# Gates and branches multiplied by token, two slots a pair of 512 columns, merged branches turned for the output projection

## The reference, cut to what matters

```python
for layer in range(2):
    h = rms_norm_2(x, norm1_g[layer])
    y_sb    = stick-breaking attention of h @ w_l[...]      # 256 wide
    y_rwkv  = rwkv7 time mix of h @ w_l[...]                # 256 wide
    y_moba  = moba attention of h @ w_l[...]                # 256 wide
    y_hgrn  = hgrn2 mixer of h @ w_l[...]                   # 256 wide
    merged = None
    for n, y_n in enumerate((y_sb, y_rwkv, y_moba, y_hgrn)):
        gate = sigmoid(h @ w_l[:, GATE_OFF + n * 1024 : GATE_OFF + (n + 1) * 1024])
        term = gate * (y_n @ w_branch[layer, n])            # (256, 256) @ (256, 1024)
        merged = term if merged is None else merged + term
    x = x + merged @ w_out[layer]                           # (256, 1024) @ (1024, 1024)
    h2 = rms_norm_2(x, norm2_g[layer])
    x = x + (silu(h2 @ w_ffn_gate) * (h2 @ w_ffn_up)) @ w_ffn_down
```

## Time and profile before

| | |
|---|---|
| median of three runs | 1333.72 us (1331.26 to 1333.73) |
| the profiled execution | 1330.48 us, of it the span 1328.7 us |
| PE busy | 1282.2 us (97%), 10548 matmuls |
| PEld busy | 1160.2 us (87%) |
| DVE busy | 837.4 us (63%) |
| ACT busy | 692.6 us (52%) |
| POOL busy | 118.6 us (9%) |
| DMA | 222.93 MB, 168 GB/s on average |
| mean granted clock of PE | 0.992 of full speed |

### The profile page before, as it was taken

How to read it: one execution, slowest core, us unless ns; L and a number is a source line. 1 busy time by engine, 2 the same in 40 slices (tenths; PEclk the granted TensorE clock), 3 DMA queues, 4 the chain that set the end, 5 groups by cost and what they waited for, 6 DMA issues and landing times.

```text
span 1328.7 us, 24883 instructions
## 1 busy us (share of the span) xinstructions
PE 1282.2 (97%) x10548; PEld 1160.2 (87%) x10548; DVE 837.4 (63%) x1257; ACT 692.6 (52%) x894; POOL 118.6 (9%) x77
## 2 busy tenths in 40 slices
PE   5999999999999999999999999999999999999997
PEld 4998898889999999989888888999999889888886
DVE  3567756886656977656655544556878756755533
ACT  2455536765766566244544434766567335544432
POOL 0000000000001330232000000000430130100000
PEclk9999999999999999999999999999999999999999
DMA  9766745724434433124555554434443114555552
GB/s 387 261 255 258 288 181 177 257 85 159 157 128 159 159 128 127 66 96 159 189 178 176 186 190 158 150 136 142 150 154 127 65 67 160 206 176 178 185 167 86
DMA packets 35102, 222.93 MB, mean 168 GB/s; under 512 B 3888, under 2 KB 8240, under 8 KB 9264
## 3 DMA queue, kind: packets, MB, share of 16 engines
q1 hardware_dynamic: 30384, 215.05, 45.8%
q10 hardware_dynamic: 4608, 6.29, 1.4%
HBM read 220.28 MB, written 1.05 MB: 167 GB/s over the span
## 4 chain that ended last, share of the span: by engine, by line
PE 85%; DVE 8%; ACT 4%; DMA 1%; issue 1%; SPq 0%; POOL 0%; ACTq 0%; DVEq 0%
PE pj L612 56%; PE yv L612 13%; PE sc L612 9%; PE tp L612 5%; DVE ring_rounded L711 3%; ACT w_split L702 1%; PE tp L481 1%; DMA big<-weights 1%; PE tp L1767 1%; DVE big L1730 1%; DMA ring<-weights 1%; DVE att_area L555 1%; DVE rw L1555 0%; ACT att_area L511 0%; DVE yT_rounded L1722 0%
## 5 line engine op out<-in xcount | busy, mean ns | idle before, releaser
L711 DVE TENSOR_TENSOR ring_rounded<-ring,w_split 128x2048 fp32r<-128x2048 f32 x108 | 256.2, 2375 | 57.5 <-ACT w_split L702 55.2
L702 ACT CAST w_split<-ring 128x2048 fp32r<-128x2048 f32 x108 | 205.4, 1902 | 43.7 <-PE pj L612 27.5
L1979 DVE TENSOR_TENSOR ring_rounded<-ring,big_rounded 128x2048 fp32r<-128x2048 f32 x62 | 142.1, 2293 | 102.4 <-ACT big_rounded L1862 102.3
L612 PE MATMUL pj<-h_split,w_split 128*128 128x256 f32 x1264 | 175.5, 292 | 5.1 <-DVE h_split L2317 2.1
L612 PEld LDWEIGHTS pj<-h_split,w_split 128*128 128x128 f32 x1264 | 159.7, 194 | 13.5 <-issue 9.2
L612 PE MATMUL pj<-h_split,ring_rounded 128*128 128x256 f32 x1264 | 163.7, 282 | 2.0 <-DVE ring_rounded L711 2.0
L612 PEld LDWEIGHTS pj<-h_split,ring_rounded 128*128 128x128 f32 x1264 | 155.5, 188 | 3.2 <-DVE ring_rounded L711 2.8
L1862 ACT CAST big_rounded<-ring 128x2048 fp32r<-128x2048 f32 x66 | 125.8, 1907 | 50.8 <-PE pj L612 49.2
L612 PE MATMUL pj<-hT_rounded,w_split 128*128 128x256 f32 x1136 | 148.1, 283 | 0.0
L612 PEld LDWEIGHTS pj<-hT_rounded,w_split 128*128 128x128 f32 x1136 | 141.6, 192 | 0.0
L1236 POOL TENSOR_TENSOR big<-big 128x512 f32<-128x512 f32 x16 | 31.0, 1940 | 737.2 <-DVE big L1169 725.0
(11 more groups left out here) (366 smaller groups left out, 2214.8 us busy)
## 6 DMA issues: line engine op xcount, KB each, us to landing
ring<-weights SPq DMA_DIRECT2D x180, 1024.0 KB, 4.9
big<-weights SPq DMA_DIRECT2D x20, 1024.0 KB, 7.4
first_block<-biases ACTq DMA_DIRECT2D x32, 192.0 KB, 5.3
xT<-x_t SPq DMA_DIRECT2D x1, 1024.0 KB, 9.2
out_t<-scr SPq DMA_DIRECT2D x4, 256.0 KB, 2.9
con<-constants SPq DMA_DIRECT2D x1, 896.0 KB, 6.6
aux<-small SPq DMA_DIRECT2D x1, 832.0 KB, 10.3
level_masks_sb<-levels SPq DMA_DIRECT2D x1, 672.0 KB, 9.1
```

Source lines behind the costliest of these rows:

```text
L612: return nc.tensor.matmul(out, lhsT, rhs, start=start, stop=stop, skip_group_check=True)
L702: act.post(nc.scalar.copy(w_split[:, w % 2], ring[:, in_ring(idx)]), s["w_high"])
L711: dve.post(nc.vector.tensor_tensor(ring_r[:, at], ring[:, at], w_split[:, w % 2].bitcast(F32), ALU.subtract), s["w_low"])
L1979: e.tell(engine.tensor_tensor(w_low(t, i), w, value(w_high(i)), ALU.subtract), signal)
```

## The change

The gates and branches of the second block are multiplied by token. A pair of gate slots (0 and 1, 2 and 3, ...) now holds 512 output columns, the first slot for input chunks 0 to 3 and the second for chunks 4 to 7. `pe_gate` takes 128 tokens of the activations as stationary operand and 512 columns of weights as moving one: 2 token halves x 3 terms x 4 chunks = 24 matmuls of 128x512 a slot, token half T into bank n+T; both banks stay open over the two slots of a pair. All three terms of token half 0 run before those of token half 1. ACT evacuates only at a pair's second slot, with two tanh: the first after the signal `gate_first`, the second after `slot_done`. A gate in `big2` is a quarter q: 512 columns (half q // 2) of 128 tokens (half q % 2). A branch's quarter is cut the same way, 6 matmuls of 128x512 (branch 1: 2 fp32 products). Gate 6 and gate 7 are cut between their token halves.

The merged sum now lies by token, so it is turned for the output projection: `pe_merged_turn` does 8 transposes of 128x128 for each half of the columns, the first half before the last quarter of branch 1, the second half between out0 and out1. ACT casts and DVE subtracts from PSUM. The first halves (chunks 0 to 3) of out0 and out1 run before the second halves of both; out2 and out3 are as before. Some semaphores are shared (`sums_ready`, `turned`) in place of two that each had before.

```diff
+gate_part = lambda n: int(n.split("gate")[1])
...
+    if "gate" in n:
+        return 2 * (1 - gate_part(n) % 2)
     return 4 if "branch" in n else 0 if "down" in n or "ffn" in n else 1
...
-        gates = big2[:, :].rearrange("p (n m t) -> p n m t", n=4, t=SEQ)
+        gate_at = lambda n, q: big2[:, (4 * n + q) * 512:(4 * n + q + 1) * 512]
...
+            if "gate" in name and gate_part(name) % 2:
+                name = f"{name.split('gate')[0]}gate{gate_part(name) - 1}"
...
+        def pe_gate(pe, name, Ts=(0, 1)):
+
+            idx, half, n = IDX[name], gate_part(name) % 2, bank_use(name)
+            high, low = (ap.rearrange("p (k n) -> p k n", n=2 * SEQ)
+                         for ap in (w_split[:, ORDINAL[idx] % 2], ring_r[:, in_ring(idx)]))
+            if 0 in Ts:
+                arrived(pe.eng, idx)
+                pe.take(s["w_high"])
+            for T in Ts:
+                bank = pj[(n + T) % NPJ]
+                if half == 0:
+                    pe.eng.wait_ge(bank_free[(n + T) % NPJ], (n + T) // NPJ)
+                for i, (h, w) in enumerate(((hh, high), (hT_r, high), (hh, low))):
+                    if i == 2 and T == 0:
+                        pe.take(s["w_low"])
+                    for k in range(KC // 2):
+                        last = matmul(bank[:, :], h[:, half * (KC // 2) + k, T * P:(T + 1) * P], w[:, k],
+                                      half == i == k == 0, half == 1 and i == 2 and k == KC // 2 - 1)
+                if T == 1:
+                    last.then_inc(slot_done, 1)
+                elif half == 1:
+                    last.then_inc(s["gate_first"].sem, 1)
...
-            pe_split(pe, f"L{layer}gate6", ks=range(KC // 2))
+            pe_gate(pe, f"L{layer}gate6", (0,))
             pe.take(s["rwkv_y_copied"])
             matmul(sc[1][:, :], C("head_ones"), flat(r_at)).then_inc(s["rwkv_mean"].sem, 1)
-            pe_split(pe, f"L{layer}gate6", ks=range(KC // 2, KC))
+            pe_gate(pe, f"L{layer}gate6", (1,))
             pe.take(s["rwkv_dev"])
             pe_head_sums(tp[0], r_bt, s["rwkv_var"])
-            pe_split(pe, f"L{layer}gate7", between=lambda: pe_rwkv_spread(pe))
-
-        def pe_rwkv_spread(pe):
+            pe_gate(pe, f"L{layer}gate7", (0,))
             pe.take(s["head_scale"])
             pe_head_spread(tp[1], rwkv_roots, s["head_spread"])
+            pe_gate(pe, f"L{layer}gate7", (1,))
...
-            e.eng.wait_ge(bank_free[n % NPJ], n // NPJ + 1)
+            for use in (n, n + 1) if "gate" in name else (n,):
+                e.eng.wait_ge(bank_free[use % NPJ], use // NPJ + 1)
...
-                for m in range(2):
-                    for k in range(2):
-                        last = matmul(bank_of(name)[:, m * SEQ:(m + 1) * SEQ], w[:, k, (2 * q + m) * P:(2 * q + m + 1) * P],
-                                      y[:, 2 * n + k], i == m == k == 0, i == len(terms) - 1 and k == 1)
+                half, T = q // 2, q % 2
+                for k in range(2):
+                    last = matmul(bank_of(name)[:, :], y[:, 2 * n + k, T * P:(T + 1) * P],
+                                  w[:, k, half * 512:(half + 1) * 512], i == k == 0, i == len(terms) - 1 and k == 1)
             last.then_inc(slot_done if q == 3 else s["branch_sums"].sem, 1)
...
-            pair = gates[:, n, 2 * q:2 * q + 2]
-            free(dve, nc.vector.scalar_tensor_tensor(flat(pair), flat(pair), 1.0, b[:, :], ALU.add, ALU.mult), name)
+            gate = gate_at(n, q)
+            free(dve, nc.vector.scalar_tensor_tensor(gate, gate, 1.0, b[:, :], ALU.add, ALU.mult), name)
+
+        turned_bank = lambda pair: (sc + yv)[pair]
+
+        def pe_merged_turn(pe, half):
+
+            pe.take(s["merged"], 2)
+            for pair in (2 * half, 2 * half + 1):
+                for c in range(2):
+                    at = (2 * (pair % 2) + c) * P
+                    for T in range(NT):
+                        last = nc.tensor.transpose(turned_bank(pair)[:, c * SEQ + T * P:c * SEQ + (T + 1) * P],
+                                                   gate_at(0, 2 * half + T)[:, at:at + P], C("ident"))
+                last.then_inc(s["turned"].sem, 1)
+
+        def dve_merged_low(dve, pair):
+            dve.take(s["merged_high"])
+            dve.post(nc.vector.tensor_tensor(both(scr_r, pair), turned_bank(pair)[:, :], value(both(hh, pair)),
+                                             ALU.subtract), s["merged_low"])
...
-                total = flat(gates[:, 0, 2 * q:2 * q + 2])
+                total = gate_at(0, q)
                 evacuated(pool, f"L{layer}branch0.{q}")
                 for n in (2, 3):
                     evacuated(pool, f"L{layer}branch{n}.{q}")
-                    ins = nc.gpsimd.tensor_tensor(total, total, flat(gates[:, n, 2 * q:2 * q + 2]), ALU.add)
+                    ins = nc.gpsimd.tensor_tensor(total, total, gate_at(n, q), ALU.add)
...
-            GATES.update({f"{t}gate{i}": flat(gates[:, i // 4, 2 * (i % 4):2 * (i % 4) + 2]) for i in range(16)})
+            GATES.update({f"{t}gate{i}": [gate_at(i // 4, i % 4 - 1 + T) for T in range(NT)] for i in range(1, 16, 2)})
...
             elif name in GATES:
-                b = done(act, name)
-                free(act, nc.scalar.activation(GATES[name], b[:, :], ACT.Tanh, scale=0.5), name)
+                n = bank_use(name)
+                for T, dst in enumerate(GATES[name]):
+                    if T == 0:
+                        act.take(s["gate_first"])
+                    else:
+                        done(act, name)
+                    b = (n + T) % NPJ
+                    nc.scalar.activation(dst, pj[b][:, :], ACT.Tanh, scale=0.5).then_inc(bank_free[b], 1)
+                    act.eng.wait_ge(bank_free[b], (n + T) // NPJ + 1)
...
+                    if q == 3:
+                        pe_merged_turn(pe, 0)
                     pe_branch(pe, f"{t}branch1.{q}")
-                for i in range(KC // 2):
-                    pe_split(pe, f"{t}out{i}", (hh, scr_r), (s["merged_high"], s["merged_low"], 2) if i == 0 else None)
+                for half in range(2):
+                    pe.take(s["merged_high"], 2)
+                    pe.take(s["merged_low"], 2)
+                    for i in range(2):
+                        if half == 0 and i == 1:
+                            pe_merged_turn(pe, 1)
+                        pe_split(pe, f"{t}out{i}", (hh, scr_r), ks=range(half * (KC // 2), (half + 1) * (KC // 2)))
+                        if half == i == 1:
+                            pe_squares(pe, 0, squares)
+                for i in range(2, KC // 2):
+                    pe_split(pe, f"{t}out{i}", (hh, scr_r))
                     if i:
...
-                for q in range(4):
-                    act.take(s["merged"])
-                    act.post(nc.scalar.copy(flat(hh[:, 2 * q:2 * q + 2]), flat(scr[:, 2 * q:2 * q + 2])),
-                             s["merged_high"])
+                for pair in range(4):
+                    act.take(s["turned"])
+                    act.tell(nc.scalar.copy(both(hh, pair), turned_bank(pair)[:, :]), s["merged_high"])
...
-                    two = slice(2 * q, 2 * q + 2)
-                    dve.post(nc.vector.tensor_tensor(flat(scr[:, two]), flat(gates[:, 0, two]), flat(gates[:, 1, two]),
-                                                     ALU.add), s["merged"])
-                for q in range(4):
-                    two = slice(2 * q, 2 * q + 2)
-                    dve.take(s["merged_high"])
-                    dve.post(nc.vector.tensor_tensor(flat(scr_r[:, two]), flat(scr[:, two]), value(flat(hh[:, two])),
-                                                     ALU.subtract), s["merged_low"])
+                    dve.tell(nc.vector.tensor_tensor(gate_at(0, q), gate_at(0, q), gate_at(1, q), ALU.add), s["merged"])
+                    if q == 2:
+                        for pair in range(2):
+                            dve_merged_low(dve, pair)
                 dve_lows(dve, IDX[t + "out1"])
+                for pair in (2, 3):
+                    dve_merged_low(dve, pair)
                 dve_residual_split(dve, t + "out", VEC["norm2"] + 8 * layer)
...
-        put(a["w_in_2"][layer], [t + n for n in named + numbered("gate", 16)])
+        cut = len(named) * SEQ
+        put(a["w_in_2"][layer][:, :cut], [t + n for n in named])
+        w = a["w_in_2"][layer][:, cut:].reshape(2, KC // 2, P, 8, 512).transpose(3, 0, 2, 1, 4).reshape(16, P, SLOT)
+        for name, values in zip(numbered("gate", 16), w):
+            out[IDX[t + name]] = values
```

20 lines of the change are left out of this document (11 added, 9 removed).

## The result

The changed kernel takes 1339.68 us (median of 4 runs, 1338.79 to 1343.01) against 1333.72 us for the kernel before (4 runs), a ratio of 1.0054 [1.0033, 1.0075]. A second comparison gave 1.0064 [1.0047, 1.0082]. I had forecast 1332.7 us and at most 1338.0. The profiled execution took 1340.12 us for a span of 1338.3 us.

A forecast was written before the change was run, and what follows sets the result against it. The prediction took TensorE, busy 97% of the span, to bound the kernel. Terms of -9.9, -1.2, +2.8, +4.2, +2.4 and +0.7 summed to -1.0 us, giving 1332.7 us; range 1326.5 to 1338.

The forecast's parts named there:

- gates and branches, streaming: Gate slots and branch quarters: 512-column matmuls save 13 ns per pair of 256s, -9.9 us for gates, -1.2 for branches.
- low waits at gates 3, 9, 10: Hgrn stage: low parts of weights wanted earlier, TensorE waits 0.73, 0.85 and 0.6 us; 2.1 us per layer, +4.2 us.
- gate 7: End of rwkv: TensorE waits 1.2 us per layer for the low part of gate 7's weights, +2.4 us.
- turns and output projection: Merged branches to output projection: 32 transposes cost +2.8 us, the rest of the section +0.7 us.
- Rival C: Gates and branches: 512 columns are not cheaper per column within one bank; +8.4 us, 1342 us, chance 0.07.
- the second of the signs: Hgrn steps: the forecast is wrong if a wait it doesn't name holds their chain; no size given.
- Rival A: Gates of the hgrn stage and gate 7: the early low part costs almost nothing; -6.4 us, 1327.3 us, chance 0.3.
- Rival B: Output projection paced by ACT's casts, out2 and out3 waiting, 2 us per layer; +3.0 us, 1336.7 us, chance 0.15.

The follow-up runs named there:

- e_best3: Changed kernel with tanh's table at gate 0, out3's low part after out2's residual, gates 3, 7, 9, 10 term by term over both token halves: 1331.79 us, 1.0004.
- e_table: Changed kernel plus one addition, ACT loading the table of tanh at gate 0: 1339.58 us, ratio 1.0051 to the kernel before.
- e_taborder: Changed kernel with two repairs, tanh's table loaded at gate 0 and out3's low part made after out2's residual: 1335.69 us, ratio 1.0032.
- e_seven: Changed kernel with gate 7 term by term over both token halves, the spread of head roots between second and third term: 1339.87 us, ratio 1.0059.
- e_best2: Changed kernel with tanh's table at gate 0, out3's low part after out2's residual, gates 3, 7, 9 term by term over both token halves: 1332.79 us, 1.0000.
- e_gates: Changed kernel without turns (output not the reference's), with tanh's table at gate 0 and gates 3, 7, 9 term by term over both token halves: 1328.08 us, 0.9967.
- e_order: Changed kernel with one move on DVE, out3's low part made after the residual of out2: 1337.91 us, ratio 1.0040.
- a_again: The changed kernel run once more, unaltered: 1340.13 us, ratio 1.0064 to the kernel before.

## Why the prediction was wrong

For both layers, from the table (layer 1 is like layer 0; its last stretch is longer by the same 1.6 us by its rows), in us against the forecast's sum:

```
                                      forecast   traces
gates and branches, streaming          -11.1      -5.4    e_best3, gate 0 to gate 7: -2.57 and -2.78
table load                               0        +2.3    e_table: 1.20 and 1.12
low waits at gates 3, 9, 10             +4.2      +2.5    e_best3 against e_taborder: 1.22 and 1.27
gate 7                                  +2.4      +2.3    e_seven: 1.17 each
turns and output projection             +3.5      +4.3    e_best2 against e_gates: 2.16 each
small gains at gate 7 and out0           0        -0.5    e_gates: -0.26 each
late residual, feed-forward start        0        +3.2    e_order: 1.6 each
sum                                     -1.0      +8.7    spans of a_again and before: +8.9
```

The traces' terms are differences between kernels, one repair after another, so their sum has to come near the whole; the first row is what is left with all repairs in, with the waits that these leave.

**Gates: mis-sized, the largest miss.** "121 ns for 256 columns and 230 ns for 512, 13 ns gained per pair" took both figures as slot length over number of matmuls. The 121 is that of gate 3, which has small matmuls behind it, the 230 that of a feed-forward slot which follows another slot directly and has transposes behind it; in the middle of a slot 256 columns take 0.120 us. At both edges the 512s pay 0.11 us where the 256s pay 0.06 to 0.08, and of the slots in the hgrn stage all but gates 2 and 3 have both edges. The comparison should have been between slots with the same neighbours. Rival C (no gain at all, +8.4) was wrong on the other side; the measured 0.17 to 0.20 lies between. The rule of the Trainium skill that I set against the trace ("TensorE: Matmul & The Clock Gate", "Back-to-back issue gap") would have given 1.9 us for the 768 pairs; the slots give 5.4 to 6.4, so neither it nor my 9.9 fits. That its sum came out slower than before was right for another reason. The branches were mis-sized too: of the 5.4 us the stretches from branch 0 to gate 7 have 0.5, gate 6 included, where 1.2 were forecast for the quarters alone. A quarter goes from 1.62 to 1.58 us at best (553.00 before, 552.49 after), not by 0.08, and two waits for DVE in that stretch grow by 0.06 and 0.12 us.

**Table load: missed.** I counted the tanh that leaves ACT at even slots as a gain of 0.60 us (which it isn't over a pair: odd slots have two now, and ACT is busy 692.3 us after 692.6) and didn't ask what else went with it: the term stood at nothing. TensorE's wait there is the second of the signs that I had named for a wrong forecast, a wait that I don't name. The load stood in the trace of before at 424.79, in front of gate 0's tanh, behind 2.11 us of idle time, where it cost nothing. The Trainium skill ("ScalarE: Activation LUTs", "What ACT_TABLE_LOAD costs") gives 1283 ns and another 1380 ns of drain for a switch; here the trace agrees with the first figure (1.28 us) and shows no drain, as the load begins 0.02 us behind one ACTIVATE's end and the next follows 0.01 us behind its own.

**Low waits in the hgrn stage: right places, gate 9 right, the other two too large.** In the changed kernel (a_again) gate 9 is 0.79 us longer than gate 8, 6.52 against 5.73 (idle 0.50 of it, as the idle time counts only from the end of the record before, and TensorE starts slower behind it); 0.85 was forecast. Gate 3 loses 0.3 (0.73 forecast) and gate 10 in layer 1, where nothing else holds it, 0.13 (0.6). The forecast let TensorE run ahead by the slots gained; but at gate 2 the table load held it back by 1 us. With both repairs gate 3 waits longer (5.99 us against 5.90), still not 0.73, as the lead is 0.2 per slot and not 0.31. The 0.73 and 0.85 themselves come to 0.65 and 0.77 from the figures that the prediction gives beside them. Rival A (the low part costs almost nothing) is refuted by gates 9 and 7.

**Gate 7: right.** 0.98 us of idle time and 1.17 in all for 1.2, at the place and with the releaser named.

**Turns: nearly right.** 16 in a layer cost 1.28 us by doubling, for 1.4. The wait before out0 is 0.27 us (0.7 forecast): DVE's low part of the second pair ends at 600.04, 8.2 us behind the first matmul of branch 1, and TensorE gets there at 8.0 instead of 7.7; the one before out2 0.69 (0.45).

**Rival B: its mechanism, at another place; the feed-forward start missed.** "The 2.29 us split at L711 standing before the second residual" is what happened (614.06 ahead of 616.26), and out3's cast was still ready 28.5 us behind the first matmul of branch 1, as I had it. What cost time is the same order one slot on, before the third residual. I had it decide at the first matmul of out3, and out3 starts on time (its cast ends 0.43 us before). I closed the sum there and treated the feed-forward part as unchanged. Its first casts hang on that residual, over ACT, POOL and back to DVE, and the price fell 9 and 14 us after that residual, at 631.52 and 636.77. B's +4 was near the measured +3.2; I gave it 0.15 because the lag that it needed, one operation of DVE, seemed an accident, when I had myself worked out that the cast came later.

So the error is 5.7 (streaming) + 2.3 (table) + 3.2 (residual) + 0.8 (turns), less 1.7 of low waits, 0.5 of small gains and 0.1 of gate 7: 9.7 us. In the time the loss is 7.2 to 8.5 us (the two ratios), in the traces 8.9.

What stays open: the clock fall at gate 6. It stands in 5 of 13 traces of the changed kernel and its variants (never in both layers of one), in none of two of the kernel before, and costs 1.6 us where it falls. At that rate it would add 0.6 us on average; whether it belongs to the change, two traces can't say.

## What to carry to other kernels

Price a matmul shape between the neighbours that it will have, edges included, not by a mean taken elsewhere. When an instruction leaves an engine, look at what it brought with it: a table load moves to the next user, and that may be the one place where three engines wait in turn. And when a weight buffer is given back later, follow its split, and the splits behind it, to the end of the queue they stand in: what is behind it there, not the matmul that needs it, may be late, so a consumer starting on time doesn't close the sum.

## What the runs showed of the hardware

Two executions of the kernel before have the same times to a few hundredths of a us for hundreds of us, and differ by 2.9 us at the head, ahead of gate 0 (all 14 later traces start gate 0 between 0.75 us before and 3.28 us after its time in the first). The granted clock falls there in every trace, for 3.4 to 13.7 us at a time, near 30 and 200 us. Much of the scatter of whole runs can come from that, and a stretch of a trace measures finer than a median of runs.

DVE's product of 128x256 (L2008) takes 0.35 us in twelve of 16 cases, and 3.89 or 4.74 us in the four beside POOL's 128x2048 subtraction of 4.6 us, each of which it outlasts by 0.15 us; in the kernel before the four (L1962 there) take 1.76 or 4.76 us and end 0.15 us behind POOL too (lines of one source, instructions of the tile hT after; columns are the shortest, middle and longest in ns):

```profile
L2008 DVE TENSOR_SCALAR hT<-xT,vec x16: 347/353/4743, 610.8 to 1141.7; 128x256 f32<-128x256 f32 x16
```

The Trainium skill ("GPSIMD Engine Reference", "1. Specifications") says that GpSimd's interfaces to SBUF are shared with VectorE, with contention for DVE instructions in a two-port mode or with two SBUF inputs. L2008 has one tensor as input, and no row tells in which mode it ran, so the rows fit the page only if it was the two-port one; no run here took POOL's work away to test it.
